# The cell's last chunk in halves without its state update, and the attention's first rows and weight loaded and scaled during the cell

## The reference

```
def mlstm_cell(...):            # 4 heads of 256, chunks of 128 rows
    def step(carry, inp):       # carry: c_st (256 x 256), n_st, m_st for each head
        s = (q k^T) * exp(d_log - m_t);  num = s v + g * (q c_st);  den = sum(s) + g * (q n_st)
        h = num / max(|den|, exp(-m_t))
        c_new = decay * c_st + (w_k k)^T v      # used by the next chunk only
h = rmsnorm(o * h, norm_g) + skip * xc
y = h * silu(z);  out = y @ w_out;  h1 = h0 + gate * out
# second layer
hn = rmsnorm(h1, norm_g[1]) * (1 + scale) + shift
q, k, v, z = split(hn @ od_w_in)
```

## Time and profile before

| | us |
|---|---|
| median of three runs | 2969.28 (2964.95 to 2972.94) |
| the profiled execution | 2971.52 |
| its span | 2969.7 |
| PE busy | 2764.2 (93%) |
| DVE busy | 1578.8 (53%) |
| ACT busy | 1099.4 (37%) |
| POOL busy | 642.5 (22%) |
| mean granted TensorE clock | 0.964 |

### The profile page before, as it was taken

One profiled execution on the slowest core, in us unless ns is written; L12 is line 12 of the kernel. 1 busy time (PEld: TensorE's weight loads), 2 busy tenths in 40 slices (PEclk: granted clock), 3 DMA queues, 4 the chain that ended last, 5 costly groups with the idle time before them and its releaser, 6 DMA issues. The chain is left out here.

```text
span 2969.7 us, 36829 instructions
## 1 busy us (share of the span) xinstructions
PE 2764.2 (93%) x13163; PEld 2194.4 (74%) x13163; DVE 1578.8 (53%) x3228; ACT 1099.4 (37%) x2378; POOL 642.5 (22%) x528
## 2 busy tenths in 40 slices
PE   5899998999999899799997899996999999899999
PEld 2687887888887678678886677775787777667776
DVE  6475771556655556544444666664533331456564
ACT  3612221222222332434433555553422221366664
POOL 0005652454544100133222000000000000133332
PEclk7999999999999999899998999997999999899999
DMA  8225446444454555788886465553322223522221
GB/s 279 85 77 149 145 152 146 144 147 148 144 158 138 167 212 182 255 242 265 275 258 201 142 181 158 174 165 131 95 75 79 76 85 114 163 65 86 86 88 62
DMA packets 461515, 445.07 MB, mean 150 GB/s; under 512 B 149685, under 2 KB 357901, under 8 KB 459917
## 3 DMA queue, kind: packets, MB, share of 16 engines
q1 hardware_dynamic: 357828, 337.20, 38.2%
q10 hardware_dynamic: 103504, 105.51, 10.5%
HBM read 280.98 MB, written 162.70 MB: 149 GB/s over the span
## 5 line engine op out<-in xcount | busy, mean ns | idle before, releaser
L2885 PE MATMUL a_pg<-a_hT,a_whl 128*128 128x512 f32 x640 | 257.1, 402 | 3.4 <-DVE a_whl L902 3.4
L2887 PE MATMUL a_pg<-a_hT,a_whl 128*128 128x512 f32 x640 | 252.0, 394 | 0.0
L2886 PE MATMUL a_pg<-a_hT,a_whl 128*128 128x512 f32 x640 | 251.8, 393 | 0.0
L908 PE MATMUL p_g<-hT,w_hl 128*128 128x512 f32 x512 | 212.5, 415 | 0.0
L854 PE MATMUL pg<-hT,w_hl 128*128 128x512 f32 x512 | 206.2, 403 | 6.6 <-DVE w_hl L902 6.6
L856 PE MATMUL pg<-hT,w_hl 128*128 128x512 f32 x512 | 201.5, 394 | 0.0
L855 PE MATMUL pg<-hT,w_hl 128*128 128x512 f32 x512 | 201.5, 394 | 0.0
L910 PE MATMUL p_g<-hT,w_hl 128*128 128x512 f32 x512 | 200.5, 392 | 0.0
L909 PE MATMUL p_g<-hT,w_hl 128*128 128x512 f32 x512 | 200.1, 391 | 0.0
L2885 PEld LDWEIGHTS a_pg<-a_hT,a_whl 128*128 128x128 f32 x640 | 121.9, 190 | 42.2 <-DVE a_whl L902 11.4
L2887 PEld LDWEIGHTS a_pg<-a_hT,a_whl 128*128 128x128 f32 x640 | 121.5, 190 | 26.3
(11 more groups left out here) (528 smaller groups left out, 6853.0 us busy)
## 6 DMA issues: line engine op xcount, KB each, us to landing
s_wt<-s5w_d SPq DMA_DIRECT2D x64, 354.0 KB
w_raw<-in_ev_w_in SPq DMA_DIRECT2D x32, 512.0 KB, 6.0
s5w_d<-gate_sums SPq DMA_DIRECT2D x32, 512.0 KB, 3.0
vo_d<-e_stage ACTq DMA_DIRECT2D x64, 256.0 KB, 3.9
shared<-h_d SPq DMA_DIRECT2D x28, 512.0 KB, 4.1
ada_w<-in_ada_w SPq DMA_DIRECT2D x32, 384.0 KB, 8.1
a_raw<-in_od_w_in SPq DMA_DIRECT2D x40, 256.0 KB, 3.5
gate_sums<-h_d SPq DMA_DIRECT2D x18, 512.0 KB, 4.0
```

What stands on the lines that cost most here:

```text
L908: nc.tensor.matmul(out, w(0, k), x(0, k), start=(k == 0), stop=False)
L2885: mm(bank, w[:, 0, k, :], x[:, 0, k, :], start=(k == 0), stop=False)
L2886: mm(bank, w[:, 0, k, :], x[:, 1, k, :], start=False, stop=False)
L2887: last = mm(bank, w[:, 1, k, :], x[:, 0, k, :], start=False, stop=(k == KC - 1))
```

## The change

In the cell, the last chunk's state product (TensorE) and state update (VectorE) are left out, with the waits that belonged to them. `inverse(15)` moves ahead of `residual(14, 1)`. `turn` waits for the heads one by one, for every chunk. Chunk 15's blend, high part, low part and output matmuls are done in two halves of four row blocks: `blend_last`, `rest_last` and `outputs_last` take the place of `blend`, `y_part` and `outputs`. The root for the first four row tiles is computed in chunks 11 and 12, SP loads these tiles after chunk 8's work, and VectorE scales two in chunk 13 and two in chunk 14. The attention's first weight part is loaded behind the loop of SP, ahead of the last two stores. The block no longer waits for the stores; the wait stands in `attend_in`, ahead of the fourth block's rows. There, block 0's rows and part 0's weight are taken where the cell left them, the rows of blocks 1 and 2 are loaded first, block 3 goes partly where block 0's rows were, and the four steps of the root (now for 12 columns) stand ahead of block 1's scaling. `f`, the evacuated tile, takes the place of `qa`; GpSimd's masks wait for `w_lo`.

```diff
+                    if c == 8:
+                        sp.wait_ge(wo_lo, KC)
+                        for j in range(4):
+                            sp.wait_ge(h_out[j % 2], 16 * (j // 2 + 1))
+                            sp.dma_start(m.first_rows[j], m.h1_d.rearrange("(c t) d -> c t d", t=MC)[j]).then_inc(m.rows_in, 16)
+                sp.wait_ge(s_done, seq(LAST, 0))
+                sp.wait_ge(b_done, seq(LAST, 0))
+                wz = a["od_w_in"][0].rearrange("(k p) (c a r d) -> c r p k a d", p=P, a=2, r=4, d=AD)[3, 0]
+                for x in range(2):
+                    sp.dma_start(m.first_raw[:, :, AD * x:AD * (x + 1)], wz[:, :, x]).then_inc(m.raw_in, 16)
                 store(NMC - 2)
                 store(NMC - 1)
-                for j in range(2):
-                    sp.wait_ge(h_out[j], 16 * NMC // 2)
                 sp.wait_ge(gate_out, 16)
...
-                        act.wait_ge(c_done, i - 1)
+                        act.wait_ge(c_done, min(i - 1, seq(LAST, 0)))
...
+                    if c == 12:
+                        act.wait_ge(mean_ready, 1)
+                        nc.scalar.activation(m.stat[:, 2, 0], m.stat[:, 1, 0], ACT.Sqrt).then_inc(sd_ready, 1)
...
-                y_part(LAST)
+                for j in range(2):
+                    act.wait_ge(y_ready, 2 * LAST + j + 1)
+                    if j == 0:
+                        act.wait_ge(o_done, 2 * LAST)
+                    nc.scalar.copy(yhl[:, 0, 4 * j:4 * j + 4], yf[:, 4 * j:4 * j + 4]).then_inc(y_hi, 1)
...
+                def row_scales():
+                    v.wait_ge(sd_ready, 1)
+                    rsqrt_steps(nc, L, *(m.stat[:, r, 0] for r in (1, 2, 3, 4)))
+
+                def scale_row(j):
+                    if j == 0:
+                        v.wait_ge(m.rows_in, 64)
+                    ts(m.first_rows[j], m.first_rows[j], m.stat[:, 3, 0, j:j + 1], None, ALU.mult).then_inc(rows_scaled, 1)
+
+                def blend_last(j):
+                    ks = slice(4 * j, 4 * j + 4)
+                    if j == 0:
+                        v.wait_ge(xs_ready, LAST + 1)
+                        v.wait_ge(y_lo, LAST)
+                        v.wait_ge(y_hi, LAST)
+                    v.wait_ge(h_turned, 2 * LAST + j + 1)
+                    for k in range(4 * j, 4 * j + 4):
+                        g = ROWS["m_norm_g"] + k
+                        last = stt(out=yf[:, k, :], in0=O[j][:, (k % 4) * MC:(k % 4 + 1) * MC], scalar=m.cols[:, g:g + 1], in1=xs[:, k, :],
+                                   op0=ALU.mult, op1=ALU.add)
+                    last.then_inc(t_read, 1)
+                    v.wait_ge(z_in, 16 * (LAST + 1))
+                    v.wait_ge(t_read, 2 * LAST + j + 1)
+                    tt(yf[:, ks, :], yf[:, ks, :], zt[:, ks, :], ALU.mult).then_inc(y_ready, 1)
+
+                def rest_last(j):
+                    ks = slice(4 * j, 4 * j + 4)
+                    v.wait_ge(y_ready, 2 * LAST + j + 1)
+                    v.wait_ge(y_hi, LAST + j + 1)
+                    tt(yhl[:, 1, ks], yf[:, ks], yhl[:, 0, ks].bitcast(F32), ALU.subtract).then_inc(y_lo, 1)
...
+                    if c == 11:
+                        v.wait_ge(h_squared, 4)
+                        ts(m.stat[:, 1, 0], m.stat[:, 0, 0], 1.0 / D, EPS, ALU.mult, ALU.add).then_inc(mean_ready, 1)
+                        v.wait_ge(mean_ready, 1)
...
-                    state(c, 0)
+                    if c < LAST:
+                        state(c, 0)
                     output(c, 0)
                     if c:
                         inverse(c - 1)
                     weight_of(c, 1)
+                    if c == 12:
+                        row_scales()
+                    if c in (13, 14):
+                        scale_row(2 * (c - 13))
+                        scale_row(2 * (c - 13) + 1)
                     if c >= 2:
                         residual(c - 2, 1)
                         blend(c - 1)
...
-                state(LAST, MH - 1)
                 variance(LAST)
+                inverse(LAST)
                 residual(LAST - 1, 1)
-                inverse(LAST)
-                blend(LAST)
-                y_part(LAST)
+                blend_last(0)
+                rest_last(0)
+                blend_last(1)
+                rest_last(1)
                 for n in range(2):
                     residual(LAST, n)
+                v.wait_ge(rows_scaled, 4)
...
-                    pe.wait_ge(kw_ready, i + 1)
+                    if c < LAST:
+                        pe.wait_ge(kw_ready, i + 1)
                     if h == 0:
                         pe.wait_ge(*((v_in[j], 32 * ((c + 1) // 2)) if c else (m.ahead, 16 * 11)))
-                    if i:
-                        pe.wait_ge(c_ready, 2 * i)
-                    mm(C0[:, 0:HW], kw[h % 2][:, 0:P], vo[j][:, h, 0:HW], start=True, stop=True)
-                    mm(C1[:, 0:HW], kw[h % 2][:, P:2 * P], vo[j][:, h, 0:HW], start=True, stop=True).then_inc(c_done, 1)
+                    if c < LAST:
+                        if i:
+                            pe.wait_ge(c_ready, 2 * i)
+                        mm(C0[:, 0:HW], kw[h % 2][:, 0:P], vo[j][:, h, 0:HW], start=True, stop=True)
+                        mm(C1[:, 0:HW], kw[h % 2][:, P:2 * P], vo[j][:, h, 0:HW], start=True, stop=True).then_inc(c_done, 1)
                     pe.wait_ge(st_ready, i + 1)
                     if i:
                         pe.wait_ge(ha_ready, i)
                     mm(AA[:, 0:HW], st[h % 2][:], vo[j][:, h, 0:HW], start=True, stop=True).then_inc(a_done, 1)
 
                 def turn(c):
-                    pe.wait_ge(h_ready, MH * (c + 1))
                     hf = hs[c % 2][:].rearrange("p h e -> p (h e)")
                     if c == 0:
                         pe.wait_ge(gate_copied, 1)
                     for k in range(KC):
+                        if k % 2 == 0:
+                            pe.wait_ge(h_ready, MH * c + k // 2 + 1)
...
+                def outputs_last():
+                    for j in range(2):
+                        pe.wait_ge(y_lo, LAST + j + 1)
+                        for n in range(2):
+                            if j == 0:
+                                pe.wait_ge(t_read, 2 * LAST + n + 1)
+                            cols = slice(n * 512, (n + 1) * 512)
+                            for k in range(4 * j, 4 * j + 4):
+                                mm(O[n][:], yhl[:, 0, k, :], wo[:, 0, k, cols], start=(k == 0), stop=False)
+                                mm(O[n][:], yhl[:, 0, k, :], wo[:, 1, k, cols], start=False, stop=False)
+                                last = mm(O[n][:], yhl[:, 1, k, :], wo[:, 0, k, cols], start=False, stop=(k == KC - 1))
+                            if j:
+                                last.then_inc(o_done, 1)
...
-        f = [reg[:, 2048 + 512 * j:2560 + 512 * j] for j in range(2)]
-        xt = [[xring[:, j] for j in range(4)], [xring[:, 4 + j] for j in range(4)], [xring[:, j] for j in range(4)],
-              [m.spare[:, 0:D], m.spare[:, D:2 * D], reg[:, 0:D], reg[:, D:2 * D]]]
+        f = qa
+        xt = [m.first_rows, [xring[:, 4 + j] for j in range(4)], [xring[:, j] for j in range(4)],
+              [m.spare[:, 0:D], m.spare[:, D:2 * D], m.first_rows[0], m.first_rows[1]]]
+        raw_of = lambda n: raw if n else m.first_raw
...
                 for j in range(4):
-                    sp.dma_start(xt[0][j], hv[0, :, j]).then_inc(x0_in[j], 16)
-                weights(0)
+                    sp.dma_start(xt[1][j], hv[1, :, j]).then_inc(x_in[1], 16)
+                weights(1)
                 for j in range(4):
-                    sp.dma_start(xt[1][j], hv[1, :, j]).then_inc(x_in[1], 16)
-                for j in range(4):
-                    sp.dma_start(xt[3][j], hv[3, :, j]).then_inc(x_in[3], 16)
-                weights(1)
+                    sp.dma_start(xt[2][j], hv[2, :, j]).then_inc(x_in[2], 16)
                 for h in range(2):
                     for j, name in enumerate(("od_q_norm_g", "od_k_norm_g")):
                         sp.dma_start(gain[AD * h:AD * (h + 1), j:j + 1], a[name].rearrange("o d -> d o"),
                                      allow_slow_non_contiguous=True).then_inc(gain_in, 16)
                 sp.wait_ge(turned, KC)
+                for j in range(2):
+                    sp.wait_ge(m.h_out[j], 16 * NMC // 2)
                 for j in range(4):
-                    sp.dma_start(xt[2][j], hv[2, :, j]).then_inc(x_in[2], 16)
+                    sp.dma_start(xt[3][j], hv[3, :, j]).then_inc(x_in[3], 16)
                 weights(2)
...
-                    act.wait_ge(w_in, 32 * (n + 1))
+                    act.wait_ge(*((w_in, 32 * n) if n else (m.raw_in, 32)))
                     if n >= 2:
                         act.wait_ge(g_done, unit[n - 2, NB - 1] + 1)
-                    split_weights_hi(nc, act, raw, whl[n % 2]).then_inc(w_hi, 1)
```

(19 more changed lines are left out.)

24 lines of the change are left out of this document (14 added, 10 removed).

## The result

The changed kernel took 2952.47 us (median of five, 2948.46 to 2953.22) where the kernel before took 2968.06 (2964.95 to 2972.94): ratio of the runs 0.9939, 95% interval 0.9928 to 0.9949, which is 18.1 us less (15 to 21); the two medians themselves differ by 15.6. Run again beside the experiments it came to 0.9927 and 0.9931. The forecast was 2948.4, its range 2942 to 2956.

The account below looks back on a forecast made before the run. TensorE, busy 93% of the span, was taken as the bound. Terms 3.1 + 6.0 + 1.8 + 1.5 + 9.6 - 0.8 - 0.3 = 20.9 us off the median 2969.3 gave 2948.4, range 2942 to 2956.

Parts of the forecast that it names:

- A: Rival, tail and attention: clock falls (term 1.0), hand-overs dear (tail 4.5), contention 1; gain 17.9 us, 2951.4; chance 0.22.
- C: Rival: tail shortened, but VectorE's added work uncovered (3.8 us) and barrier still costs the store (1.5); 2953.7; chance 0.08.
- Chunk 15 without its state: Last cell chunk: dropping state products gains 2.2 us at head 0, 0.9 at head 3, nothing at heads 1 and 2; 3.1.
- Tail in halves: Cell's end: the wait before the last 48 output matmuls shrinks from 10.0 to 4.0 us; gain 6.0.
- The level of the clock: Cell's last 48 matmuls: all may run at 2.4 GHz, gaining 2.6 us; treated as a coin, 1.8 taken.
- Store not awaited: Barrier between cell and attention: block starts after ScalarE's last square, not the last store's landing; gain 1.5 us.
- Rows and weight ahead: Attention's start: rows and weight come scaled, so block start to first product takes 10.2 us, not 19.8; gain 9.6.
- Root exposed: Attention, ahead of block 1's scaling: inverse root of blocks 1 to 3 now delays TensorE; cost 0.8 us.
- Contention: Attention's block: GpSimd's memsets beside VectorE's subtraction and first splits slow one operation; cost 0.3 us, bounds 0 and 1.5.
- B: Rival: shorter pause keeps clock high in first double steps, the 48 matmuls and later products; gain 25.7 us, 2943.6; chance 0.10.
- D: Rival: chunk 15 gains only at head 3; fourth block's rows or third weight stall 8 us; gain 10.7 or less; chance 0.05.
- E: Rival, attention's interleaved stage: TensorE keeps the lower clock for all four blocks, losing 34 us; slower, 2982; chance 0.03.

Follow-up runs that it names:

- the third: Changed kernel unaltered, run again beside the kernels with chunk 15's hole filled, against the kernel before: 2953.59 us, ratio 0.9931.
- the first: Changed kernel as first measured and profiled, against the kernel before: median 2952.47 us, ratio 0.9939; the profiled execution took 2948.46.
- the second: Changed kernel unaltered, run again beside the early-root and tail-fill kernels, against the kernel before: 2949.30 us, ratio 0.9927.
- The last experiments: Changed kernel plus early root and idle TensorE work at tail, barrier and block 0: 2942.96 us (0.9906); with chunk 15's hole filled too: 2946.56 (0.9908).

## Why the prediction was right, and what in it was not

The time lay 4.1 us above the forecast, inside the range and 3.5 us from its upper end. By the stages the change gave 18.2 to 19.0 us against 20.9 in the sum. By time alone the rivals A (2951.4) and C (2953.7) lie nearer than the forecast. Term by term:

- **Chunk 15 without its state**: 3.1 foreseen; of the three profiles of the changed kernel it is 3.1 in the third, 2.6 in the first and 0.9 in the second. What was missed is the hole. The prediction said that the removed matmuls of heads 1 and 2 bring nothing, and stopped there. They had kept TensorE at work while it waited for VectorE's sum; without them it stands for 1.9 us. Where the clock falls behind it, as in the second, that loses 1.5. Another 0.5 in the first and 0.6 in the second went earlier, in chunk 14: the subtraction beside GpSimd's operation, shown above, took 2.16 and 2.32 us, and TensorE waited 1.01 and 1.17. In the third it took 1.23 and TensorE did not wait. The prediction named new idle time in chunks 9 to 14 as a sign of being wrong; but this one comes and goes in the same kernel, and the profile before has such slow subtractions as well (1.7 to 2.3 us in five of 16 chunks).
- **Tail in halves**: 6.0 foreseen, 5.8 measured, alone and in the whole.
- **The level of the clock**: this is the step that failed. "With one gap of 4.0 us holding eight transposes in place of 10.0 us, all 48 may run at 2.4 GHz", and half of 2.6 plus a loss was taken, 1.8. The clock fell in all six profiles that have the short gap unfilled. Their 48 took 12.54 to 13.90, mean 13.0; those behind the long gap 13.02 to 13.69, mean 13.4. The term is 0.35 on average, and -0.3 in the profile shown. Its price for a fall was too low as well: "some 8 matmuls run low, 1.6 lost", where a fall costs 1.4 to 2.8 against the 11.11 with the clock held. The row it leaned on, a gap of 3.3 us with the level kept in the earlier trace rows, showed only that the clock had not fallen *yet*. Here it fell at 2030.2, 3.7 us after the last dense matmul had started, and stayed low into the next ones; in two of the six profiles it fell only 1.1 and 1.2 us into the 48. The prediction quoted the Trainium skill ("TensorE: Matmul & The Clock Gate", Part 1) for a switch that comes at a different matmul from run to run; there it is the switch up. The profiles agree as far as the length of the low stretch goes (the 48 spread over 1.4 us in the same kernel), and behind the 1.9 us hole also on whether it comes at all. At the tail it was no coin: six of six.
- **Store not awaited**: 1.5 foreseen, 1.62 measured. The barrier does not need the store to have landed: in the profile after, the last store landed at 2048.60, and the block had begun at 2048.48.
- **Rows and weight ahead**: 9.6 foreseen, 9.7 measured. The cast starts 0.66 into the block (0.85 foreseen), and from the cast to the first product it is 9.35 (9.4).
- **Root exposed**: -0.8 foreseen, -0.88 measured.
- **Contention**: -0.3 foreseen in the attention's block, 0 there. The weight's subtraction took 1.23 beside memsets. The Trainium skill ("SBUF — State Buffer", section on the two separate sides) had it so, and the trace agrees with it, as it does in chunk 14, where GpSimd read two tiles and the subtraction took 2.16. That the mean takes 0.51 beside a memset, and 0.97 in four of the experiments, stays unexplained.
- **Work added in the cell**: 0 foreseen, 0 measured. The periods from chunk 8 to chunk 13 are 26.2 to 26.7 us in both profiles.

With the first profile's sizes, 2.6 + 5.8 - 0.3 + 1.6 + 9.7 - 0.9 = 18.5, against 18.6 by the stages. Of the rivals, A had the clock's fall right, though not its price (1.0 for the term, 0.35 found), but the hand-overs were not dear (4.5 put on the tail, 5.8 found), and no contention of 1 us stood in the block. That its time fits best is in part luck. In B the idea that a shorter pause between the blocks lifts the front is false: the clock was 0.50 there. The last experiments made it 1.00, and then the front gave 0.4 to 0.7 us, not the 1.4 that B put on it (11 less 9.6). C falls with the store and the cell's chunks, D with head 0's gain and with the third weight: TensorE waits 3.44 us for its split in the profile before and the same 3.44 in the one after. E falls as well: once dense work began the clock came back, and over 2065 to 2100 it is 0.96.

## What to carry to other kernels

Work taken off an engine that is waiting anyway gains nothing and may cost: it opens a hole, and the clock fell behind this one in three of seven profiles. Idle matmuls in a pause held the clock at the tail, at no cost in the length of the gap; that they do so in the hole is likely, not shown. A pause that is halved need not bring the clock back, so read a level that is to be kept from the dense work *behind* such a pause, not from the first microseconds within it. And when a chain is moved ahead, look for what is left in its old place directly in front of the next wait: four small steps there cost 0.9 us, and moving them with the scaling behind them was worth 3.5.

## What the runs showed of the hardware

The granted clock falls after a pause has begun and not with it, and even after it has ended. In the tail it was still 1.00 through 3.7 us of thin work and fell just before the first dense matmul; in chunk 15 of the second profile it fell 0.65 us into dense work, behind the hole of 1.9. The low stretch then lasted 3.4 us there and 6.8 us in the tail shown (3.4 in four of the six with the short gap), nearly all of it with TensorE busy without a gap.

In block 0 the clock was 0.50 in the profile after and 1.00 with the fills. The runs do not tell whether the matmuls ahead of the barrier or the transposes within the block did it.

A block's barrier costs 1.4 us, from the end of the read behind the last square (2046.91 + 0.19 = 2047.10) to the first instruction behind it (2048.48), and it does not wait for a store that is still under way (this one landed at 2048.60).

In the cell, VectorE's subtraction of the low part (two tiles read, 1.23 us alone) and GpSimd's operation on two tiles (1.27 alone) get in each other's way, and the one that starts second pays. In chunk 14 the subtraction took 2.16 us, begun 0.19 behind GpSimd's, and 2.32 in another profile of the same kernel, begun 0.02 behind it. Where the subtraction began first it took 1.23, and GpSimd's operation up to 2.35. Beside memsets the subtraction takes 1.23.
